# The norm scale behind the products in all four feed-forward stages of a two-layer encoder, on one core

## The reference, cut to what matters

```python
def rms_norm(x, g):
    y = xf * lax.rsqrt(jnp.mean(xf * xf, axis=-1, keepdims=True) + EPS)
    return (y * g.astype(jnp.float32)).astype(x.dtype)

def swiglu(h, w_gate, w_up, w_down):
    return (jax.nn.silu(h @ w_gate) * (h @ w_up)) @ w_down

        h = rms_norm(x, ffn1_norm_pre[l])
        h = swiglu(h, ffn1_w_gate[l], ffn1_w_up[l], ffn1_w_down[l])
        x = x + 0.5 * rms_norm(h, ffn1_norm_post[l])
```

## Time and profile before

| | |
|---|---|
| median of 3 runs | 958.1 us (957.89 to 958.3) |
| the profiled execution's own time | 957.9 us |
| its span in the trace | 956.1 us |
| TensorE busy | 945.5 us (99%), in 5355 products |
| VectorE busy | 668.7 us (70%) |
| ScalarE busy | 528.7 us (55%) |
| granted clock of TensorE | 0.999 of full speed |
| chain that ended last, by engine | PE 91%, DVE 6%, ACT 2% |

### The profile page before, as it was taken

How to read it: one execution, slowest core, us unless ns; L and a number is a source line. 1 busy time by engine, 2 the same in 40 slices (tenths; PEclk the granted TensorE clock), 3 DMA queues, 4 the chain that set the end, 5 groups by cost and what they waited for, 6 DMA issues and landing times.

```text
span 956.1 us, 13180 instructions
## 1 busy us (share of the span) xinstructions
PE 945.5 (99%) x5355; PEld 824.3 (86%) x5355; DVE 668.7 (70%) x963; ACT 528.7 (55%) x703; POOL 25.2 (3%) x44
## 2 busy tenths in 40 slices
PE   8999999999999999999999999999999999999997
PEld 8888888889987888888888888888899888888886
DVE  6966867777788866656688666657768887665654
ACT  7645544558776645445565454445587565544542
POOL 0300000000000012000000000000000000000000
PEclk9999999999999999999999999999999999999999
DMA  9688556456424767665466656555554366565541
GB/s 311 202 261 288 176 191 205 132 194 225 154 89 139 261 216 200 199 196 179 153 205 219 212 178 206 189 178 198 184 190 133 102 205 199 185 206 182 184 168 44
DMA packets 131627, 180.30 MB, mean 189 GB/s; under 512 B 4088, under 2 KB 114824, under 8 KB 131568
## 3 DMA queue, kind: packets, MB, share of 16 engines
q1 hardware_dynamic: 129216, 175.65, 56.0%
q0 software_dynamic: 2192, 3.76, 1.8%
q10 hardware_dynamic: 160, 0.07, 0.0%
HBM read 178.40 MB, written 2.63 MB: 189 GB/s over the span
## 4 chain that ended last, share of the span: by engine, by line
PE 91%; DVE 6%; ACT 2%; issue 1%; DVEq 0%
PE UP L430 30%; PE Y L457 25%; PE UP L435 16%; PE UP L734 7%; PE Y L445 3%; DVE wlo L1133 1%; PE Y L489 1%; PE UP L469 1%; PE Y L491 1%; PE Y L495 1%; ACT junk L840 1%; PE Y L511 1%; DVE logit L1401 1%; DVE xs L1197 1%; DVE x L1202 0%
## 5 line engine op out<-in xcount | busy, mean ns | idle before, releaser
L1133 DVE TENSOR_TENSOR wlo<-raw,whi 128x2048 fp32r<-128x2048 f32 x152 | 347.8, 2291 | 136.5 <-ACT whi L823 136.4
L823 ACT ACTIVATE whi<-raw 128x2048 fp32r<-128x2048 f32 x159 | 304.2, 1914 | 93.0 <-DMA raw<-in_ffn_w_gate 71.7
L430 PE MATMUL UP<-xT,whi 128*128 128x512 f32 x1280 | 304.8, 390 | 0.0
L430 PEld LDWEIGHTS UP<-xT,whi 128*128 128x128 f32 x1280 | 237.4, 188 | 47.5
L457 PE MATMUL Y<-whi,yT 128*128 128x512 f32 x736 | 206.5, 391 | 0.0
L435 PEld LDWEIGHTS UP<-xT,wlo 128*128 128x128 f32 x1280 | 164.1, 191 | 6.2
L435 PE MATMUL UP<-xT,wlo 128*128 128x256 f32 x1280 | 166.0, 283 | 0.0
L457 PEld LDWEIGHTS Y<-whi,yT 128*128 128x128 f32 x736 | 135.1, 188 | 25.6
L457 PE MATMUL Y<-wlo,yT 128*128 128x512 f32 x368 | 113.6, 390 | 0.0
L925 ACT ACTIVATE gate_small<-UP 128x512 f32<-128x512 f32 x40 | 23.8, 596 | 112.6 <-PE UP L435 112.4
L734 PE MATMUL UP<-xT,whi 128*128 128x256 f32 x448 | 82.2, 285 | 0.0
(11 more groups left out here) (212 smaller groups left out, 807.0 us busy)
## 6 DMA issues: line engine op xcount, KB each, us to landing
raw<-in_ffn_w_up SPq DMA_DIRECT2D x44, 1024.0 KB, 5.4
raw<-in_ffn_w_down SPq DMA_DIRECT2D x44, 1024.0 KB, 5.0
raw<-in_ffn_w_gate SPq DMA_DIRECT2D x43, 1024.0 KB, 5.3
raw<-in_w_in SPq DMA_DIRECT2D x20, 1024.0 KB, 5.3
raw<-in_w_out SPq DMA_DIRECT2D x8, 1024.0 KB, 5.0
gains<-in_ffn_norm_post SPq DMA_DIRECT2D x4, 512.0 KB, 6.0
shift_scratch<-shift_rows POOLq DMA_DIRECT2D x1, 1536.0 KB, 12.3
gains<-in_ffn_norm_pre SPq DMA_DIRECT2D x3, 512.0 KB, 6.5
```

Of the source, the lines that this page charges most:

```text
L430: nc.tensor.matmul(bank(UP, b + c), h[:, kt, c * P:c * P + P], xT[:, kt, :, :].rearrange("p h s -> p (h s)"), start=kt == 0, stop=False, s ...
L823: A.activation(whi[:, k % RING, :], raw[:, k % RING, :], ACT.Copy).then_inc(hi_ready, 1)
L1133: V.tensor_tensor(wlo[:, k % RING, :], raw[:, k % RING, :], whi[:, k % RING, :].bitcast(F32), ALU.subtract).then_inc(lo_ready, 1)
```

## The change

Stages 2, 3 and 5 now do what stage 0 did. In their entries `weigh_x` multiplies by the gain alone and stands directly behind each `add_y`. The scale of the norm in front is made later: on VectorE behind `turned_lo(s, 0, 1)` for token half 0, and behind `turned_lo(s, 1, 1)` for half 1 (`feed_scale`, the former `first_scale`); on ScalarE the root of half 0 stands behind `turned_hi(s, 0, 1)` and in front of the squares of half 1, and the root of half 1 behind the last `turned_hi`. In the stage itself, two products spread the scales over a row, VectorE copies the row once and multiplies 20 sums by it. `ones`, which lay in a tile that the mixer uses, has its own tile now.

```diff
 def root_number(s, t, kind):
     if s == 0:
         return t
-    return 4 * s - 2 + (t if s == STAGES else 2 * t + kind)
+    if s == STAGES:
+        return 4 * s - 2 + t
+    return 4 * s - 2 + (2 * t + kind if s % 3 == 1 else 2 * kind + t)
...
+            def spread_scale(s):
+
+                for t in range(NT):
+                    pe.wait_ge(scale_ready, 2 * ffn_number(s) + t + 1)
+                    mm = nc.tensor.matmul(SCALE_ROW[:, t * P:t * P + P], ones[:, :], diagonal[:, t, :], start=True, stop=True)
+                mm.then_inc(scale_spread, 1)
...
                 gate_unit(1)
+                if s:
+                    spread_scale(s)
                 turn_first_pair()
...
             def enter(s):
 
+                feed = s % 3 != 1
                 for t in range(NT):
+                    if t:
+                        act.wait_ge(x_squared, quarter(s, 0, 1) + 1)
                     square_y(s, t, 0)
                     if t:
                         turned_hi(s, 0, 0)
...
                     norm_root(s, t, POST)
                     if t:
                         turned_hi(s, 0, 1)
+                        if feed:
+                            norm_root(s, 0, PRE)
                     for h in range(2):
                         square_x(s, t, h)
-                    norm_root(s, t, PRE)
+                    if not feed:
+                        norm_root(s, t, PRE)
                 for h in range(2):
                     turned_hi(s, 1, h)
+                if feed:
+                    norm_root(s, 1, PRE)
...
-                V.scalar_tensor_tensor(xs[:, t, feature_half(h)], x[:, t, feature_half(h)], rs[:, t, PRE:PRE + 1],
-                                       gains[:, 0, feature_half(h)], ALU.mult, ALU.mult).then_inc(xs_ready, 1)
+                dst, src, gain = xs[:, t, feature_half(h)], x[:, t, feature_half(h)], gains[:, 0, feature_half(h)]
+                if s % 3 == 1:
+                    V.scalar_tensor_tensor(dst, src, rs[:, t, PRE:PRE + 1], gain, ALU.mult, ALU.mult).then_inc(xs_ready, 1)
+                else:
+                    V.tensor_tensor(dst, src, gain, ALU.mult).then_inc(xs_ready, 1)
...
                 for h in range(2):
                     add_y(s, t, h)
+                    if s < STAGES and s % 3 != 1:
+                        weigh_x(s, t, h)
...
-                    if s == 0:
-                        scaled(gate, gate_sum, i).then_inc(gate_scaled, 1)
+                    scaled(gate, gate_sum, i).then_inc(gate_scaled, 1)
...
-                    if s == 0:
-                        scaled(up, up_sum, i).then_inc(up_scaled, 1)
+                    scaled(up, up_sum, i).then_inc(up_scaled, 1)
```

More of the change, by code:

```diff
@@ L177, in program @@
         gain_cols = sb("gain_cols", [P, KT])
+        ones = sb("ones", [P, P])
         onehot, vec, table = prob[0:32, 0:SHIFTS], prob[0:8, 512:512 + SHIFTS], prob[0:32, 1000:1008]
@@ L256, in wait_tile_copied @@
             eng.wait_ge(tile_copied, tile_number(l, u, t) + 1)
-        ones, gain_rows = att[:, 2, :], att[0:KT, 3, :]
+        gain_rows = att[0:KT, 3, :]
         diagonal, scale_row = att[:, 0:2, :], lg[:, 0, :]
@@ L421, in keep_clock @@
                 for _ in range(n):
-                    nc.tensor.matmul(bank(Y, 1, 0, P), ones, ones, start=True, stop=True)
+                    nc.tensor.matmul(bank(Y, 1, 0, P), ones[:, :], ones[:, :], start=True, stop=True)
             def feature_unit(b, k):
@@ L553, in enter_first @@
                 second_unit(1)
[L554 to L557, removed]
+                spread_scale(0)
             def enter(s, first_signal):
@@ L914, in token_tanh @@
                         act.wait_ge(unit_used, ffn_unit(s, "up", 0) + 1)
-                    if s == 0:
-                        act.wait_ge(scale_ready, t + 1)
-                    A.activation(tanh[:, t, :], bank(Y, 2 * t, 0, UC), ACT.Tanh, scale=half_scale[:, t:t + 1] if s == 0 else 0.5).then_inc(tok_tanh, 1)
+                    act.wait_ge(scale_ready, 2 * f + t + 1)
+                    A.activation(tanh[:, t, :], bank(Y, 2 * t, 0, UC), ACT.Tanh, scale=half_scale[:, t:t + 1]).then_inc(tok_tanh, 1)
                 def first_hidden_hi():
@@ L927, in gate_parts @@
                     lead()
-                    act.wait_ge(gate_sum if s else gate_scaled, pair_number(s, i) + 1)
+                    act.wait_ge(gate_scaled, pair_number(s, i) + 1)
                     if i == 1:
@@ L1235, in pre, with feed_scale @@
                     weigh_x(s, t, h)
-            def first_scale(t):
+            def feed_scale(s, t):
                 scale = rs[:, t, PRE:PRE + 1]
-                norm_scale(0, t, PRE)
+                norm_scale(s, t, PRE)
                 V.tensor_scalar(half_scale[:, t:t + 1], scale, 0.5, None, ALU.mult)
@@ L1252, in enter_first @@
                 split_first(0)
-                first_scale(0)
+                feed_scale(0, 0)
                 turned_lo(0, 1, 0)
@@ L1260, in enter_first @@
                 V.tensor_scalar(vec[:, :], UP[0:8, 0:SHIFTS], 1.0 / SCALE, None, ALU.mult).then_inc(vec_copied, 1)
-                first_scale(1)
+                feed_scale(0, 1)
             def enter(s):
@@ L1266, in enter @@
                 post(s, 0)
-                pre(s, 0)
+                if s % 3 == 1:
+                    pre(s, 0)
                 split_half(stage_unit(s, 1), 1)
@@ L1270, in enter @@
                 turned_lo(s, 0, 1)
-                pre(s, 1)
+                if s % 3 == 1:
+                    pre(s, 1)
+                else:
+                    norm_base(s, 0, PRE)
+                    feed_scale(s, 0)
                 turned_lo(s, 1, 0)
                 turned_lo(s, 1, 1)
+                if s % 3 != 1:
+                    norm_base(s, 1, PRE)
+                    feed_scale(s, 1)
             def ffn(s):
@@ L1279, in token_hidden @@
                     dve.wait_ge(tok_tanh, 2 * f + t + 1)
-                    half = half_square[:, t:t + 1] if s == 0 else 0.5
                     link(V.scalar_tensor_tensor(gate[:, t, :], tanh[:, t, :], 1.0, bank(Y, 2 * t, 0, UC), ALU.add, ALU.mult))
-                    V.scalar_tensor_tensor(hid[:, t, :], gate[:, t, :], half, bank(Y, 2 * t, UC, 2 * UC), ALU.mult, ALU.mult).then_inc(tok_hid, 1)
+                    V.scalar_tensor_tensor(hid[:, t, :], gate[:, t, :], half_square[:, t:t + 1], bank(Y, 2 * t, UC, 2 * UC), ALU.mult, ALU.mult).then_inc(tok_hid, 1)
                 def first_hidden_lo():
@@ L1287, in first_hidden_lo, with spread_copy @@
                                     hidden(0)[:, :, 0, :].bitcast(F32), ALU.subtract).then_inc(hid_lo, 1)
+                def spread_copy():
+                    dve.wait_ge(scale_spread, f + 1)
+                    link(V.tensor_copy(scale_row, SCALE_ROW))
                 def hidden_lo(i):
@@ L1315, in up_parts @@
                                     up_small[:, :, :], ALU.add).then_inc(up_sum, 1)
-                    if s == 0:
-                        scaled(up, up_sum, i).then_inc(up_scaled, 1)
+                    scaled(up, up_sum, i).then_inc(up_scaled, 1)
                     dve.wait_ge(swished, pair_number(s, i) + 1)
-                    dve.wait_ge(up_sum if s else up_scaled, pair_number(s, i) + 1)
+                    dve.wait_ge(up_scaled, pair_number(s, i) + 1)
                     if i == 1:
@@ L1328, in ffn @@
                 if s == 0:
-                    dve.wait_ge(scale_spread, 1)
-                    link(V.tensor_copy(scale_row, SCALE_ROW))
+                    spread_copy()
                 split(stage_unit(s, 4))
                 split(stage_unit(s, 5))
+                if s:
+                    spread_copy()
                 for i in range(1, PAIRS):
@@ L1527, in mixer @@
                 split_half(stage_unit(s, 14), 1)
-            V.memset(ones, 1.0).then_inc(ones_set, 1)
+            V.memset(ones[:, :], 1.0).then_inc(ones_set, 1)
             V.memset(epsb[:, :], EPS).then_inc(eps_set, 1)
```

## The result

The changed kernel takes 961.38 us (median of 8 runs, 960.53 to 961.76), the kernel before 958.0 in the same comparison (8 runs, 957.32 to 958.46): a ratio of 1.0033, 95% interval 1.0024 to 1.0042. The change costs 3.4 us. The forecast was 960.4, slower, by 2.4.

A forecast was written before the change was run, and what follows sets the result against it. TensorE, busy nearly all the time, was taken as the bound. Spreading products +1.32 and entries +1.11 gave +2.4 on 957.9 (profiled) or 958.1 (median), so 960.4; the forecast's own range 959.6 to 961.4, with rivals 957.7 to 962.6.

The forecast's parts named there:

- The spreading products: Two products between gate unit 1 and the transposes of hid, uncovered on TensorE, 0.44 us in each of three stages: +1.32.
- The wait for xs goes: In entries 2, 3 and 5, xs is ready before TensorE comes, so its wait (0.38 us in stage 2) is gone.
- The two stops that take its place: Entries: TensorE waits for VectorE's turned_lo within its last eight products, then for ScalarE's copy; both ways meet within 0.03 us.
- ScalarE's queue: Stage 2 entry: half 0's root holds half 1's squares and copies, moving the first product from 302.80 to 303.24: +0.44.
- The size of an entry: First product on half 1 comes later by 0.44 us in stages 2 and 5, 0.23 in stage 3: +1.11 together.
- TensorE's own stop: Stage 2 entry: fifth of the last eight products waits for turned_lo(0,1); transposes start at 301.87, ScalarE could copy at 302.56.
- Twenty scale products a stage, cost nothing: VectorE's products by the scale row, 0.69 us each, 13.8 more in all, were taken as covered: nothing.
- The first pair's slack: In each new stage the first gate sum is done 1.15 us before gate unit 2 wants it: costs nothing.
- The wait that goes with nothing in its place: Rival on the entries: product 0.38 to 0.58 us earlier, -1.34, offsetting the spreading: 957.9 to 958.1; chance 0.22.
- the rival's condition on `base_sum` of half 0: The rival with nothing in the wait's place holds if VectorE makes half 0's base_sum before about 300.0.
- VectorE late for gate unit 2: Rival: VectorE's queue slips by one split more (2.3 us), 1.15 a stage remain, +3.4 more, 963.8; chance 0.14.
- The halved throughput of the old weighing: Rival on the entries: plain products take 0.35 us less each than the old weighing, two on the chain: 958.2; chance 0.03.

The follow-up runs named there:

- run 4: Kernel before, with ones in its own tile and two unused products of ones with the identity behind gate unit 1 in stages 2, 3, 5: 959.28 us.
- run 1: Changed kernel with ScalarE's root of half 0 behind its last copies and VectorE's feed_scale of half 0 behind turned_lo(1,1): 961.6 us.
- run 2: Changed kernel with VectorE's turned_lo(0,1) between the first weighing and the second add of half 1 in the three entries: 960.68 us.
- run 3: Changed kernel with the edits of run 1 and run 2 together: 958.1 us, ratio 0.9998 to the kernel before.
- run 7: Changed kernel without VectorE's multiplications of gate and up sums by the scale row in stages 2, 3, 5: 961.44 us.
- run 5: Changed kernel with turned_lo(0,1) early as in run 2 and half 0's whole scale made where the kernel before made it: 958.01 us.
- run 6: The kernel of run 5 with half 0's spreading product moved between the transposes of half 1 and the first product on it: 957.31 us.

## Why the prediction was right

The forecast was 960.4 with a range of its own of 959.6 to 961.4; 961.38 lies at its upper edge. The mechanism held: the wait that goes, the two stops that take its place, the price of the spreading products, and VectorE's cover. Where the sum was +2.43, the rows give 3.1: the spreading products as forecast, the entries 1.76 instead of 1.11. The 0.3 that the medians have on top stay open.

**The spreading products.** 0.44 us a stage on the chain, 1.32: the rows show 0.44, and alone they cost 1.2 us (run 4; the interval of its ratio is 0.4 to 2.2 us).

**The wait for xs goes.** Right: no wait of L472 in stages 2, 3 and 5.

**The two stops that take its place.** Right, with the joint condition: "taking away either alone would win nothing" is what run 1 shows for ScalarE's queue, and nearly what run 2 shows for `turned_lo` (0.16 an entry); run 3 takes both and wins 3.3. By this, the order of the entry costs 3.3 us, and the wait for `xs` that the change removes is worth 0.42 an entry on the distance (run 3 against before).

**The size of an entry.** This term was mis-sized: 0.44 forecast in stages 2 and 5, 0.65 measured; 0.23 and 0.46 in stage 3. As a distance, 5.77 was forecast and 5.98 measured. Runs 1 and 2 take the two stops apart. With ScalarE's queue alone left (run 2) the distance is 5.82, near the 5.77 of that path; the root comes 0.13 later than forecast, and what follows it takes 0.08 less. With TensorE's own stop alone left (run 1) it is 5.99, where the numbers of the prediction give 5.74 (302.56 + 0.65 - 297.47). So TensorE's stop is the mis-sized one, and it is the later of the two by 0.16, not their equal. Three rows correct it. The weighing starts 0.86 after the start of the add it waits for (298.16 to 299.02), not 0.78, twice on the way: 0.16. From the first of the four products behind the stop to the transposes it is 1.03 (301.83 to 302.86), not 0.91: 0.12. From the transposes to the copy it is 0.63 (302.86 to 303.49), not 0.69, since no wait lies among them: -0.06. Together they are 0.22 of the 0.24 (5.98 against 5.74).

**Twenty scale products a stage, cost nothing.** Right (run 7). **The first pair's slack** was 1.15 forecast, 1.4 measured; no wait of gate unit 2 appears.

**The rivals.** The wait that goes with nothing in its place was forecast at 957.9 to 958.1: that is run 3, 958.1, and run 5, 958.0, which meets the rival's condition on `base_sum` of half 0; so the rival had the size right and the order of this kernel wrong. VectorE late for gate unit 2 didn't happen. The halved throughput of the old weighing is refuted by rows of the same size: the plain product of the new weighing takes 0.69 (299.02), the add, which has a scalar and two fp32 tensors as the old weighing had, 0.75.

## What to carry to other kernels

When work is moved off a chain, list what it now stands in front of on each engine: here an instruction that nobody needed for microseconds (the root of half 0's scale) waited 4.4 us at the head of ScalarE's queue, and a short one that TensorE needed at once (`turned_lo`) came behind two others. Two stops that end at nearly the same time hide each other; remove both before judging either. And extra products on the bounding engine cost their full length (0.44 a stage) unless they lie where that engine waits anyway, which run 6 does with one of two.

## What the runs showed of the hardware

A TensorE stop costs more than the wait that the profile lists. By run 3, the 0.79 of wait at L498 stood for 1.07 of the distance. Two things make up the other 0.28. Four products of 128x512 in a stream start 0.91 before the next group, but show 1.07 to their visible end (row 299.97), and the listed wait begins at that end: 0.16. And the four behind the stop take 1.03 until the next group starts instead of 0.91: 0.12. In the chain, which counts the first group behind a stop from its start to its visible end, both show as 1.19 to 1.20 against 0.91 to 0.93, in all the profiles that were read.

ScalarE did not take ready work ahead of a waiting instruction: its squares, ready at 300.38, started at 302.13, behind the root that had waited 4.37 us.

The first transposes of the program took between 0.60 and 1.06 us for four in profiles of kernels that are alike there. The rows around them in the changed kernel's timeline show what changes:

```profile
1.07 4.64 PE L425 MATMUL Y<-ones 128*128 128x128 f32 x20 [1.07 <-DVE ones L1560]
...
7.40 1.95 PE L425 MATMUL Y<-ones 128*128 128x128 f32 x16
```

Twenty products take 4.64 us, 0.23 each, and sixteen of the same shape behind the transposes 1.95, 0.12 each: TensorE's pace doubles in between. The transposes themselves start 0.21 apart up to 7.17 us and 0.11 apart after it; in the kernel before they start 0.11 apart from 5.78 us on. So where the pace doubles sets how long they take. The granted clock's column does not show it: it reads 1.00 from 5 to 8 us in the profiles of before and after alike.
